# Expert stage of a two-block layer: gated values transposed one expert later, and eight landing slots for expert weights in place of the residual rows

## What is computed

```
h        = rmsnorm(x) * g_ffn
group    = argmax(h @ w_r1 + b_r1)                 # 4 groups, one per token
experts  = top 2 of the group's 4 experts, weighted # 16 experts in all
hid_e    = silu(h @ w_gate[e]) * (h @ w_up[e])      # 1024 -> 256
out      = x + sum_e combine[:, e] * (hid_e @ w_down[e])   # 256 -> 1024
```

## Time and profile before

| | |
|---|---|
| median of 3 runs | 1804.76 us (1797.23 to 1806.16) |
| profiled execution, own time | 1809.09 us |
| its span, first to last instruction | 1807.3 us |
| PE busy | 1551.9 us, 86% |
| ACT, DVE, POOL busy | 697.4, 663.2, 565.9 us |
| mean granted clock of TensorE | 0.905 |

### The profile page before, as it was taken

How to read it: one execution, slowest core, us unless ns; L and a number is a source line. 1 busy time by engine, 2 the same in 40 slices (tenths; PEclk the granted TensorE clock), 3 DMA queues, 4 the chain that set the end, 5 groups by cost and what they waited for, 6 DMA issues and landing times. The chain is left out here.

```text
span 1807.3 us, 18918 instructions
## 1 busy us (share of the span) xinstructions
PE 1551.9 (86%) x7008; PEld 1196.6 (66%) x7008; DVE 663.2 (37%) x1377; ACT 697.4 (39%) x1182; POOL 565.9 (31%) x253
## 2 busy tenths in 40 slices
PE   4998999998699797995899599979997588979777
PEld 3776666666577476574778487767876366667655
DVE  2286343223201322499542223142222543332333
ACT  4542224113334644433464424543222334343451
POOL 2264210003234122242223246512441444444460
PEclk9999998558899898997999799999998889999988
DMA  3221101002122021121112224311321144444451
GB/s 128 70 82 59 46 26 37 14 12 67 41 82 93 13 82 47 48 93 53 47 53 88 71 99 129 117 47 53 100 73 53 47 136 145 140 141 140 141 188 47
DMA packets 96001, 142.10 MB, mean 79 GB/s; under 512 B 11649, under 2 KB 46648, under 8 KB 95896
## 3 DMA queue, kind: packets, MB, share of 16 engines
q1 hardware_dynamic: 92948, 136.21, 23.4%
q10 hardware_dynamic: 2660, 4.45, 0.8%
q0 software_dynamic: 288, 0.02, 0.0%
HBM read 138.55 MB, written 2.10 MB: 78 GB/s over the span
## 5 line engine op out<-in xcount | busy, mean ns | idle before, releaser
L764 POOL TENSOR_TENSOR w_lo<-raw,w_hi 128x1024 fp32r<-128x1024 f32 (+1 forms) x191 | 456.3, 2406 | 1059.9 <-ACT w_hi L1424 1059.8
L1424 ACT ACTIVATE w_hi<-raw 128x1024 fp32r<-128x1024 f32 (+1 forms) x191 | 191.9, 1032 | 231.9 <-PE ps L816 207.7
L814 PE MATMUL ps<-w_hi,act_hi 128*128 128x512 f32 (+1 forms) x560 | 230.8, 412 | 14.5 <-ACT dq L1562 6.6
L815 PE MATMUL ps<-w_lo,act_hi 128*128 128x512 f32 (+1 forms) x560 | 222.4, 397 | 0.0
L816 PE MATMUL ps<-w_hi,act_lo 128*128 128x512 f32 (+1 forms) x560 | 221.4, 395 | 0.0
L814 PE MATMUL ps<-w_hi,mix_hi 128*128 128x512 f32 x432 | 181.6, 420 | 8.9 <-DVE mix_lo L1959 8.2
L815 PE MATMUL ps<-w_lo,mix_hi 128*128 128x512 f32 x432 | 174.2, 403 | 0.0
L816 PE MATMUL ps<-w_hi,mix_lo 128*128 128x512 f32 x432 | 173.9, 403 | 0.0
L814 PEld LDWEIGHTS ps<-w_hi,act_hi 128*128 128x128 f32 (+1 forms) x560 | 106.0, 189 | 53.9 <-issue 12.6
L816 PEld LDWEIGHTS ps<-w_hi,act_lo 128*128 128x128 f32 (+1 forms) x560 | 105.8, 189 | 25.7
L814 PE MATMUL ps<-act_hi,w_hi 128*128 128x512 f32 (+5 forms) x288 | 110.3, 385 | 14.5 <-POOL w_lo L764 9.8
(11 more groups left out here) (462 smaller groups left out, 2671.5 us busy)
## 6 DMA issues: line engine op xcount, KB each, us to landing
raw<-in_w_in SPq DMA_DIRECT2D x92, 512.0 KB, 3.4
raw<-in_w_gate SPq DMA_DIRECT2D x64, 256.0 KB, 3.0
raw<-in_w_up SPq DMA_DIRECT2D x64, 256.0 KB, 3.8
raw<-in_w_down SPq DMA_DIRECT2D x32, 512.0 KB, 4.5
raw<-in_w_out SPq DMA_DIRECT2D x16, 512.0 KB, 3.5
raw<-in_w_mem_kv SPq DMA_DIRECT2D x16, 512.0 KB, 3.8
raw<-in_w_o_gla SPq DMA_DIRECT2D x8, 512.0 KB, 3.5
raw<-in_w_o_dsa SPq DMA_DIRECT2D x8, 512.0 KB, 3.4
```

The costliest lines, as they stand in the source:

```text
L764: pool.tensor_tensor(lo[:, 0:a], raw[:, g % RAW_SLOTS, 0:a], hi[:, 0:a].bitcast(F32), ALU.subtract).then_inc(*POOL.done(("w_lo", g)))
L814: pe.matmul(dst, l_hi, r_hi, start=start, stop=False, skip_group_check=skip)
L815: pe.matmul(dst, l_hi, r_lo, start=False, stop=False, skip_group_check=skip)
L1424: nc.scalar.activation(split_slot(g)[0][:, 0:a], raw[:, g % RAW_SLOTS, 0:a], ACTF.Copy).then_inc(*ACT.done(("w_hi", g)))
```

## The change

1. **The turn moves one expert on.** PE no longer turns `hid` at the end of its own visit. It turns it in the middle of the next expert's up product for the same slot (ahead of block k = 4), and the down product that reads it follows at the end of that visit. ACT's copy to `hid_hi` and DVE's `hid_lo` move along and stand first in their share of that visit. At the end of a group the turn stands in `finish`, which now comes behind `visit(v + 4)` instead of ahead. `hid` gets four buffers, `e_silu` has one instead of two.
2. **Eight landing slots.** Expert weights also land in `raw_more`, four more slots, which take the place of `x1`. SP stores `x1` to the output tensor in DRAM once the last block product has been added, waits for that and for the norm that reads `x1`, and loads it back when the last units have been split. `unsort` waits for it.
3. **Waits by unit.** PE waits for the low part of each of units 0 to 3 as it comes to it, instead of for unit 3 ahead of the visit.
4. **Routing.** `route` part 1 stands behind visit 3 instead of visit 0.

`skip` is adapted to the new counts. The core of the diff, in this order: the list, the tiles, SP, PE (`turn` and `visit`), ACT (`hid_high`, which is also its share of `finish`, and `visit`), DVE (`visit` and `unsort`):

```diff
     for v in range(NT * N_EXP):
-        if v >= NT and v // NT % 4 == 0:
-            order += [("finish", v - NT)]
         if v % NT < 2:
             order += [("weights", E_UNITS * (v // NT + 1) + 3 + v % NT)]
         order += [("visit", v)]
-        if v == 0:
-            order += [("route", 1)]
+        if v >= NT and v // NT % 4 == 0:
+            order += [("finish", v - NT)]
         if v == NT - 1:
-            order += [("combine_s",)]
+            order += [("route", 1), ("combine_s",)]
...
+        raw_more = sb("raw_more", [P, RAW_SLOTS, UNIT], 113)
-        hid = sb("hid", [P, 2, D_EXP], SC + 60)
-        e_silu = sb("e_silu", [P, 2, D_EXP], SC + 62)
+        hid = sb("hid", [P, NT, D_EXP], SC + 60)
+        e_silu = sb("e_silu", [P, D_EXP], SC + 56)
...
+        def raw_at(g):
+            if g < expert_unit:
+                return g % RAW_SLOTS
+            i = (g - expert_unit) % (2 * RAW_SLOTS)
+            return i if i >= RAW_SLOTS else (expert_unit + i) % RAW_SLOTS
...
+                if raw_before[g] is not None:
+                    sp.wait_ge(*low_by(raw_before[g]).after("w_lo", raw_before[g]))
+                if g == expert_unit + RAW_SLOTS:
+                    for t in range(NT):
+                        sp.wait_ge(*DVE.after("x", "w_out21", t))
+                        sp.dma_start(out[0, P * t:P * (t + 1), :], x1[:, t, :]).then_inc(spilled, 16)
+                    sp.wait_ge(spilled, 16 * NT)
+                    sp.wait_ge(*ACT.after("ss", "ffn", NT - 1))
+                    sp.wait_ge(*DVE.after("scaled", "ffn", NT - 1))
...
+            for i in range(RAW_SLOTS):
+                sp.wait_ge(*low_by(raw_last[RAW_SLOTS + i]).after("w_lo", raw_last[RAW_SLOTS + i]))
+            for t in range(NT):
+                sp.dma_start(x1[:, t, :], out[0, P * t:P * (t + 1), :]).then_inc(x_back, 16)
...
+            def turn(v):
+                s = v % NT
+                pe.wait_ge(*DVE.after("hid", v))
+                claim(4, (ACT, ("hid_hi", v)), (DVE, ("hid_lo", v)))
+                for c in range(2):
+                    tr = pe.transpose(ps[:, 4, P * c:P * c + P], hid[:, s, P * c:P * c + P], ident[:, :])
+                tr.then_inc(*PE.done(("turn", v)))
...
                 with pe.If_ne(flag(v), 0):
-                    pe.wait_ge(*POOL.after("w_lo", g0 + 3))
                     claim(bank, (ACT, ("e_silu", v)), (DVE, ("hid", v)))
                     for k in range(KC):
+                        if k == 4 and e % 4:
+                            turn(v - NT)
+                        if k % 2 == 0:
+                            pe.wait_ge(*low_by(g0 + k // 2).after("w_lo", g0 + k // 2))
...
                     if e % 4:
-                        down(v - NT)
-                    pe.wait_ge(*DVE.after("hid", v))
-                    claim(4, (ACT, ("hid_hi", v)), (DVE, ("hid_lo", v)))
-                    for c in range(2):
-                        tr = pe.transpose(ps[:, 4, P * c:P * c + P], hid[:, v % 2, P * c:P * c + P], ident[:, :])
+                        done = down(v - NT)
...
+            def hid_high(v):
+                act.wait_ge(*PE.after("turn", v))
+                if last_turned[0] is not None:
+                    act.wait_ge(*DVE.after("hid_lo", last_turned[0]))
                 if v >= NT:
                     act.wait_ge(*ACT.after("hid_hi", v - NT))
                     act.wait_ge(*PE.after("down", v - NT))
+                last_turned[0] = v
                 nc.scalar.activation(hid_hi[:, v % NT, :], ps[:, 4, 0:D_EXP], ACTF.Copy).then_inc(*ACT.done(("hid_hi", v)))
+
+            def visit(v):
+                if v // NT % 4:
+                    hid_high(v - NT)
+                act.wait_ge(*PE.after("up", v))
+                if v:
+                    act.wait_ge(*ACT.after("e_silu", v - 1))
+                    act.wait_ge(*DVE.after("hid", v - 1))
+                nc.scalar.activation(e_silu[:, :], ps[:, v % NT, 0:D_EXP], ACTF.Silu).then_inc(*ACT.done(("e_silu", v)))
...
             def visit(v):
                 e, s = divmod(v, NT)
                 with dve.If_ne(flag(v), 0):
+                    if e % 4:
+                        hid_low(v - NT)
...
+                dve.wait_ge(x_back, 16 * NT)
```

More of the change, by code:

```diff
@@ L506, in program, with raw_slot @@
         sort_in = semaphore("sort_in")
-        w_landed = [semaphore(f"w_landed{i}") for i in range(RAW_SLOTS)]
-        landed, total = [], [0] * RAW_SLOTS
-        for g, (_, _, pieces) in enumerate(units):
-            total[g % RAW_SLOTS] += 16 * len(pieces)
-            landed.append(total[g % RAW_SLOTS])
+        w_landed = [semaphore(f"w_landed{i}") for i in range(2 * RAW_SLOTS)]
+        def raw_at(g):
[3 more added lines that the diff above has]
+            return i if i >= RAW_SLOTS else (expert_unit + i) % RAW_SLOTS
+        def raw_slot(g):
+            return raw[:, raw_at(g), :] if raw_at(g) < RAW_SLOTS else raw_more[:, raw_at(g) - RAW_SLOTS, :]
+        landed, total, raw_last, raw_before = [], [0] * 2 * RAW_SLOTS, {}, []
+        for g, (_, _, pieces) in enumerate(units):
+            total[raw_at(g)] += 16 * len(pieces)
+            landed.append(total[raw_at(g)])
+            raw_before.append(raw_last.get(raw_at(g)))
+            raw_last[raw_at(g)] = g
+        spilled = semaphore("spilled")
+        x_back = semaphore("x_back")
         const_in = semaphore("const_in")
@@ L736, in _ @@
             for g, (chunks, n, pieces) in enumerate(units):
-                if g >= RAW_SLOTS:
-                    sp.wait_ge(*low_by(g - RAW_SLOTS).after("w_lo", g - RAW_SLOTS))
-                slot = raw[:, g % RAW_SLOTS, 0:len(chunks) * n].rearrange("p (k n) -> p k n", n=n)
-                for a, b, src in pieces:
-                    sp.dma_start(slot[:, :, a:b], src).then_inc(w_landed[g % RAW_SLOTS], 16)
+                if raw_before[g] is not None:
[7 more added lines that the diff above has]
+                    sp.wait_ge(*DVE.after("scaled", "ffn", NT - 1))
+                slot = raw_slot(g)[:, 0:len(chunks) * n].rearrange("p (k n) -> p k n", n=n)
+                for a, b, src in pieces:
+                    sp.dma_start(slot[:, :, a:b], src).then_inc(w_landed[raw_at(g)], 16)
+            for i in range(RAW_SLOTS):
+                sp.wait_ge(*low_by(raw_last[RAW_SLOTS + i]).after("w_lo", raw_last[RAW_SLOTS + i]))
+            for t in range(NT):
+                sp.dma_start(x1[:, t, :], out[0, P * t:P * (t + 1), :]).then_inc(x_back, 16)
             for t in range(NT):
@@ L763, in split_low @@
                     hi, lo = split_slot(g)
[L764 removed]
+                    pool.tensor_tensor(lo[:, 0:a], raw_slot(g)[:, 0:a], hi[:, 0:a].bitcast(F32),
                                        ALU.subtract).then_inc(*POOL.done(("w_lo", g)))
@@ L1271, in visit @@
                         mm = product(ps[:, bank, :], mix_hi[:, k, rows], mix_lo[:, k, rows], wh, wl, k == 0, k == KC - 1)
-                    mm.then_inc(*PE.done(("up", v), *([("unit", g0 + i) for i in range(4)] if s == NT - 1 else [])))
+                    done = PE.done(("up", v), *([("unit", g0 + i) for i in range(4)] if s == NT - 1 else []))
+                    mm.then_inc(*done)
                     if e % 4:
-                        down(v - NT)
-                    pe.wait_ge(*DVE.after("hid", v))
-                    claim(4, (ACT, ("hid_hi", v)), (DVE, ("hid_lo", v)))
-                    for c in range(2):
-                        tr = pe.transpose(ps[:, 4, P * c:P * c + P], hid[:, v % 2, P * c:P * c + P], ident[:, :])
-                    done = PE.done(("turn", v))
-                    tr.then_inc(*done)
+                        done = down(v - NT)
                 with pe.Else():
-                    skip(done, 3 if e % 4 else 2)
+                    skip(done, 3 if e % 4 else 1)
             def finish(v):
                 with pe.If_ne(flag(v), 0):
+                    turn(v)
                     done = down(v)
                 with pe.Else():
-                    skip(done, 1)
+                    skip(done, 2)
             def unsort():
@@ L1420, in split_high @@
                     a = len(chunks) * n
-                    act.wait_ge(w_landed[g % RAW_SLOTS], landed[g])
+                    act.wait_ge(w_landed[raw_at(g)], landed[g])
                     if slot_free(g):
                         act.wait_ge(*PE.after(*slot_free(g)))
-                    nc.scalar.activation(split_slot(g)[0][:, 0:a], raw[:, g % RAW_SLOTS, 0:a], ACTF.Copy).then_inc(*ACT.done(("w_hi", g)))
+                    nc.scalar.activation(split_slot(g)[0][:, 0:a], raw_slot(g)[:, 0:a], ACTF.Copy).then_inc(*ACT.done(("w_hi", g)))
                 fill[0] = max(fill[0], upto)
@@ L1586, in resort @@
                                          scale=col("g_ffn_2", k)).then_inc(*ACT.done(("s_hi", k)))
[L1588 to L1594, removed]
+            last_turned = [None]
+            def hid_high(v):
                 act.wait_ge(*PE.after("turn", v))
```

(23 more changed lines are left out.)

## The result

| | kernel before | changed kernel |
|---|---|---|
| median, us | 1804.63 (1797.23 to 1806.16, 4 runs) | 1822.28 (1813.87 to 1823.56, 4 runs) |
| ratio, 95% interval | | 1.0102 (1.0064 to 1.0139) |
| first up product of the experts to the span's end, profiled execution | 362.0 us | 378.0 us |

The change costs 17.7 us; by the interval, 11.5 to 25. The forecast was 1830 us, +25 on the median, with 1804 to 1845 as its range and 0.73 on slower.

What follows compares the result with a forecast made beforehand. PE sets the end and ACT lets it go late. Terms 1.0 + 0 + 1.3 - 0.2 - 1.2 + 3.3 + 0.4 + 3.2 = +7.8, plus 17 half clock: +25, 1830 us; range 1804 to 1845.

Steps and rivals of the forecast that it cites:

- Landing slots: In ACT's splits: both waits for landing weight units end, 2.8 us in the expert looked at.
- rival 3: Experts: landings made ACT late, so PE runs at 8.6 us a visit; faster, about 1776 us; chance 0.06.
- The turn in mid product: Experts of groups 1 to 3: PE stands 3.1 to 4.4 us for ACT's skipped-slot copy; -0.2, +3.3, +3.2 us.
- The 4.4 us stand: Group 3: PE stands about 4.4 us at the turn; 13.4 us an expert, three 40.3 against 37.1: +3.2.
- Half clock: After nine new stands of PE, matmuls run at half clock: +17 us, bounds 0 and 27.
- Rival 1: PE's stands cost only themselves, half clock 0 to 0.6 us each: +8 to +13, 1813 to 1818 us; chance 0.15.
- Rival 2: At the turn, bank 4's claim does not bind, ACT's skipped copies come in time: 1800 to 1804 us; chance 0.12.
- rival 4: Residual rows' load on the path (+10), or half clock 3 us a stand (+10): 1840 us; chance 0.09.
- Passages: Group changes: the down product waits behind ACT's burst, one stand of about 7 us; +1.3, -1.2, +0.4 us.
- First expert and experts 1 to 3: Start of stage: later routing delays expert 1 by +1.0 us (-0.5 to +1.7); experts 1 to 3 unchanged, 57.8 us.
- Residual rows: Store and load of x1: hidden by other work, nothing; bounds 0 to +10 us.
- Waits by unit: PE's waits for low parts: POOL is ahead except at expert 15 (about 1 us); extra waits cost nothing.

Runs made afterwards that it cites:

- Experiment 1: Kernel before with eight landing slots and the store and load of x1, the turn left where it was: 1775.18 us, ratio 0.9851.
- Experiment 2: Changed kernel with four landing slots and x1 left in place; moved turn, waits by unit and later routing kept: 1854.95 us, ratio 1.0271.
- experiment 3: Changed kernel, an expert's six splits moved to two each behind slots 3, 0 and 1, not five in a row: 1801.33 us, ratio 0.9963.
- experiment 4: Changed kernel with hid_hi copied by DVE instead of ACT, ACT's copies of skipped slots gone: 1786.99 us, ratio 0.9902.
- experiment 6: Kernel before plus only the store of x1 ahead of the experts and its load behind the last unit: 1808.37 us against 1807.4, ratio 0.9991.
- experiment 7: Kernel of Experiment 1 with PE's waits for the low parts made unit by unit: 1769.01 us, ratio 0.9769.
- Experiment 5: Kernel of experiment 4 with four landing slots and x1 as in the kernel before: 1784.36 us, ratio 0.9848.

## Why the prediction was right, and where its sizes were off

**Landing slots: right.** ACT's waits for landings went, and the bottleneck is ACT's order, not its supply. Experiment 1 shows what the prediction only said in rival 3: the landings did make ACT late for the old turn. The rival fell because the turn moved, and its price was about right for the kernel it fitted: 29 us below the kernel before, where experiment 1 measured 32. By its terms that is only partly so: 52.2 us for groups 1 and 2 (measured 53.66 and 51.49), but 27 for group 3 (34.18), and only "a little" for experts 1 to 3, which gained 4.6.

**The turn in mid product: right, in place and size.** Stands forecast for group 1: 3.1 to 3.8 us, measured 2.80 to 3.54; group 2: 4.1, measured 3.69 to 4.09; group 3: 4.4, measured 3.51, 4.14 and 1.68. Group 0: none, and 1.9 us at the down product, measured 1.73 and 1.71. Experiment 2 shows that the turn's place costs, experiment 3 that ACT's burst sets the price, experiment 4 that the copy's place in ACT's queue is needed for it. The claim of bank 4 by itself was not tried: experiment 4 takes away ACT's claim and the late `hid_hi` together. That the claim binds is read from the traces: in the changed kernel the turn starts as ACT's copy of the skipped slot ends, in experiment 4 as DVE's step for it does.

**Expert 15: overlooked.** The 4.4 us stand was counted three times in group 3. Behind expert 14 no further units are left to split, so expert 15's turn waits only 1.68 us. The sum of 40.3 us should have been 37.6; measured 40.74 with its half clock.

**Half clock: the mis-sized term.** It was taken as 17 us for nine stands. Over the forecast lengths, groups 1, 2 and 3 measured 64.42 - 62.0 = 2.4, 69.72 - 64.7 = 5.0 and 40.74 - 37.6 = 3.1 us: about 10.6 us. That is half clock less what the stands were shorter than forecast (4.09, 3.69, 3.69 us in group 2 for 4.1 and more, 3.51 and 4.14 in group 3 for 4.4). Half clock by itself can be counted in the trace: behind seven of the nine stands, 63 matmuls are followed by the next one 0.2 us late, 12.6 us; behind the one ahead of 1599.15 and behind expert 15's none are. So a stand that half clock follows costs 1.8 us, as the 1.7 to 2.3 had it; what the term had wrong is that it follows nearly every stand. The clock fell below 0.9 in group 3 alone (0.95, 0.90, 0.87), not in all three as forecast.

**Rivals.** Rival 1, at most 0.6 us of half clock a stand, named a clock near 0.95 as its sign, and group 1 has it; but 12.6 us over nine stands are 1.4 each, and its +13 at most is less than the stage's +16.1. The medians alone don't refute it: their interval begins at +11.5 us. Rival 2 falls with the stands, rival 4's load with experiment 6.

**Passages: right in sum.** Forecast +1.3, -1.2, +0.4; measured +0.7, -2.2, +1.0. They hold stands of 1.84 and 5.60 us, 5.92 and 1.29, 6.75 and 0.98, in place of one of about 7. In the second and third the long one is at the `finish` turn, which the forecast had as ready early: it, too, waits for ACT's `hid_hi`.

**First expert and experts 1 to 3: right.** +1.0 and 0 forecast, -0.3 and +0.3 measured. The routing did start later, as forecast, behind the visit, and PE waited 10.4 us for `combine`.

**Residual rows: right.** Nothing, in experiment 6. The load is issued 29 us ahead of the output's store, and DVE's first addition, at 1795.46, had waited for PE and not for a transfer. SP's queue in the changed kernel:

```profile
1769.16 1.76 SPq L766 DMA_DIRECT2D x<-out  x4
1798.14 11.22 SPq L769 DMA_DIRECT2D out<-x  x4
```

**Waits by unit: priced at nothing.** For the changed kernel no run tells. Without the moved turn they may save some us (experiment 7, not settled).

**The end: overlooked, +3.5.** The last slot's turn now also stands behind ACT's copy of a skipped slot, and the low part follows it in line with nothing between. PE at the end of the stage, changed kernel:

```profile
1776.07 0.29 PE L1265 MATMUL ps<-ones 128*1 128x1 f32 x6
1778.47 0.61 PE L1290 MATMUL ps<-ident,hid 128*128 128x128 f32 x2 [2.11 <-ACT hid_hi L1632]
1780.06 0.77 PE L839 MATMUL ps<-gap_w,hid_hi 128*128 128x512 f32 x1 [0.98 <-DVE hid_lo L2463]
```

2.11 and 0.98 us of stand, and the down product that follows is at half clock throughout (0.64 granted in this stretch). In the kernel before, the end was at full clock and `unsort` was not:

```profile
1773.54:1779.45 5.91, 3.42 (x23) 2.66 (x21) 1.91 (x6) 0.38 (x1) 0.00 (x0) 1.00 0.01 1
1779.45:1807.30 27.85, 20.38 (x81) 15.04 (x78) 11.57 (x14) 5.95 (x8) 0.00 (x0) 0.85 0.19 76
```

**The account.** Forecast 7.8 + 17 = 24.8, measured 16.1 by the stage. Half clock and shorter stands together -6.4 (10.6 for 17; half clock alone is 12.6, so -4.4 and -2.0); expert 15 -2.7; first expert, experts 1 to 3 and passages -2.0 (forecast +1.5, measured -0.5); the end +3.5; `unsort` -1.3, where the granted clock was 0.94 and not 0.85. 24.8 - 6.4 - 2.7 - 2.0 + 3.5 - 1.3 = 15.9, the rest is rounding. The mechanism was right, and the sizes together 8 us too high; that they missed by no more is in part luck, as the end's +3.5, which the forecast had left out, stood against the rest.

**Expectations that missed.** Experiment 2 was 13 us above its range: fourteen stands, those of group 0 and one in each passage (5.60 to 7.27, 5.92 to 8.60, 6.75 to 9.38) among them, grew by 1.7 to 2.8 us each, 31 us in all. Its own 1.9 us an expert would have given 30 already, not 10 to 20. Experiment 4's left out that the turn would now wait for DVE's queue, a little inside a group and much in the passages. Experiment 5's took ACT's waits for landings as waits of PE, and 3.5 of 48 us were.

## What to carry to other kernels

When a dependence moves, ask when the waiting engine now reaches it, and read the releaser's queue up to that moment, skipped work included: a copy of nothing that stands behind a burst of splits still holds the bank. Deeper landing buffers pay where the engine that they feed is late for its next reader (32 us here), and nothing where it isn't (experiment 5); try the two halves of such a change apart, since one half was worth keeping. Work moved to a freer engine lands in that engine's queue: price it at the busiest point of that queue, not at the mean.

## What the runs showed of the hardware

Stands of the same length are not followed by the same clock. The 2.80 us ahead of 1577.44 was followed by matmuls 0.43 us apart (1.2 GHz, the lower of the two levels); this one, also 2.80 us and one expert on, was not, with 0.23 us between them:

```profile
1599.15 0.41 PE L1290 MATMUL ps<-ident,hid 128*128 128x128 f32 x2 [2.80 <-ACT hid_hi L1632]
1599.32 0.48 PE L839 MATMUL ps<-far_hi,mix_hi 128*128 128x512 f32 x1
1599.63 0.39 PE L840 MATMUL ps<-far_lo,mix_hi 128*128 128x512 f32 x1
1599.86 0.39 PE L841 MATMUL ps<-far_hi,mix_lo 128*128 128x512 f32 x1
```

Nor does half clock always begin at once: the stand of 3.69 us that ended at 1671.32 was followed for 1.2 us by matmuls at full clock, and then by eight 0.43 us apart. What tells the two stands of 2.80 us apart stays open. A price for half clock is therefore a share of the stands times its cost, here seven of nine times 1.8 us, and a range around that. The other point is the spread between executions of code that two programs share: ahead of the experts it was 11.3 us in these two profiles, two thirds of the effect looked for, so that spans had to be compared by stage.
